# A hybrid decoder trunk on one Trainium2 core: V's first half in a transpose bank, a reordered first unit, and ScalarE's attention program without a loop

## What is computed

```python
q = (xn @ w_q).reshape(B, S, N_HEADS, HEAD_DIM).transpose(0, 2, 1, 3)
...
s = jnp.einsum('bhqd,bhkd->bhqk', q[:, :, q0:q1], k[:, :, :q1]) * scale
s = s + c[:, :, q0:q1, None] - c[:, :, None, :q1]
s = jnp.where(mask, s, -jnp.inf)
p = jax.nn.softmax(s, axis=-1)
outs.append(jnp.einsum('bhqk,bhkd->bhqd', p.astype(v.dtype), v[:, :, :q1]))
```

## Time and profile before

| | |
|---|---|
| median of 3 runs | 2560.55 us (2559.9 to 2560.63) |
| the profiled execution's own time | 2558.25 us |
| its span, first to last instruction | 2556.4 us |
| PE busy (matmuls) | 2446.8 us, 96% |
| DVE, ACT, POOL busy | 1271.8, 786.1, 124.8 us |
| granted TensorE clock, mean | 0.980 of full speed |
| attention, first score to last product | about 1166 to 1702 us |

### The profile page before, as it was taken

How to read it: one execution, slowest core, us unless ns; L and a number is a source line. 1 busy time by engine, 2 the same in 40 slices (tenths; PEclk the granted TensorE clock), 3 DMA queues, 4 the chain that set the end, 5 groups by cost and what they waited for, 6 DMA issues and landing times.

```text
span 2556.4 us, 28698 instructions
## 1 busy us (share of the span) xinstructions
PE 2446.8 (96%) x11353; PEld 2009.7 (79%) x11353; DVE 1271.8 (50%) x1257; ACT 786.1 (31%) x1045; POOL 124.8 (5%) x80
## 2 busy tenths in 40 slices
PE   7999889999999999998999999979999999999998
PEld 5788768888888888867777777767788888888887
DVE  5767674434333434466665656553434444444344
ACT  4543542111111111145555555542211111111112
POOL 1000010000000000011110111001000000000001
PEclk9999999999999999999999999979999999999999
DMA  3111011111111111120111101021211111111111
GB/s 116 58 58 49 25 33 50 49 49 46 44 49 49 49 49 49 34 83 25 34 34 34 33 26 32 25 85 55 58 50 49 49 43 47 49 49 49 49 33 66
DMA packets 167166, 122.63 MB, mean 48 GB/s; under 512 B 5072, under 2 KB 148672, under 8 KB 167104
## 3 DMA queue, kind: packets, MB, share of 16 engines
q1 hardware_dynamic: 165360, 117.52, 15.1%
q10 hardware_dynamic: 1744, 4.32, 0.6%
HBM read 113.37 MB, written 8.45 MB: 48 GB/s over the span
## 4 chain that ended last, share of the span: by engine, by line
PE 88%; DVE 5%; ACT 3%; issue 3%; ACTq 1%; DMA 0%; POOL 0%; DVEq 0%
PE ps L619 66%; PE ps L804 8%; PE ps L915 3%; PE ps L851 3%; PE ps L838 2%; PE ps L819 1%; PE ps L667 1%; PE ps L816 1%; ACT kh L1190 1%; DVE rstd L1346 1%; DVE kv_tmp L1716 0%; PE ps L663 0%; DVE wl L1316 0%; DVE resid L1359 0%; ACT kh L1195 0%
## 5 line engine op out<-in xcount | busy, mean ns | idle before, releaser
L619 PE MATMUL ps<-xh,wh 128*128 128x512 f32 x1680 | 523.5, 393 | 10.6 <-DVE wl L1316 10.1
L619 PE MATMUL ps<-xl,wh 128*128 128x512 f32 x1680 | 518.2, 390 | 0.0
L619 PE MATMUL ps<-xh,wl 128*128 128x512 f32 x1680 | 518.0, 389 | 0.0
L619 PEld LDWEIGHTS ps<-xh,wh 128*128 128x128 f32 x1680 | 315.1, 188 | 81.4 <-issue 16.4
L1353 DVE TENSOR_TENSOR tmp<-ps,rstd 128x1024 f32<-128x1024 f32 x96 | 117.3, 1224 | 506.0 <-PE ps L619 506.0
L619 PEld LDWEIGHTS ps<-xh,wl 128*128 128x128 f32 x1680 | 315.7, 188 | 65.9
L619 PEld LDWEIGHTS ps<-xl,wh 128*128 128x128 f32 x1680 | 315.7, 188 | 65.7
L1359 DVE TENSOR_TENSOR resid<-ps,resid 128x1024 f32<-128x1024 f32 x216 | 261.6, 1222 | 187.9 <-PE ps L619 187.5
L974 ACT ACTIVATE wh<-raw 128x1024 fp32r<-128x1024 f32 x193 | 201.6, 1049 | 402.2 <-PE ps L619 349.7
L1316 DVE TENSOR_TENSOR wl<-raw,wh 128x1024 fp32r<-128x1024 f32 x193 | 238.8, 1241 | 169.6 <-ACT wh L974 169.5
L619 PE MATMUL ps<-hh,wh 128*128 128x512 f32 x704 | 219.4, 393 | 1.7 <-DVE hl L1585 1.7
(11 more groups left out here) (186 smaller groups left out, 2792.2 us busy)
## 6 DMA issues: line engine op xcount, KB each, us to landing
raw<-in_w_ffn_in SPq DMA_DIRECT2D x88, 512.0 KB, 3.8
raw<-in_w_ffn_out SPq DMA_DIRECT2D x44, 512.0 KB, 3.3
raw<-in_w_rec_in SPq DMA_DIRECT2D x16, 512.0 KB, 4.0
raw<-in_w_kvf SPq DMA_DIRECT2D x16, 512.0 KB, 3.9
xin<-in_x SPq DMA_DIRECT2D x4, 1024.0 KB, 10.1
raw<-in_w_rec_out SPq DMA_DIRECT2D x8, 512.0 KB, 4.0
raw<-in_w_q SPq DMA_DIRECT2D x8, 512.0 KB, 3.7
spill<-resid SPq DMA_DIRECT2D x8, 512.0 KB, 2.6
```

The source lines that it names most:

```text
L619: last = pe.matmul(acc[:, h], w, v[:, h], start=(first and p == 0), stop=(final and p == 2))
```

## The change

Three things change. First, step A projects into `t_ps[0]` in place of `f_alt`. PE's waits ahead of A and ahead of S1 go; instead PE waits for DVE's scaling of A ahead of T0 of the first unit, the next user of that bank. Second, the first unit's steps stand in another order: T1 comes ahead of X and Y, and S0 and S1 of the next unit's scores come ahead of V1 and T3. Third, ACT's loop over the six middle pairs becomes a Python loop, so that its instructions stand one after the other six times with constants in place of registers. The loops of PE, DVE, POOL and SP stay.

```diff
 UNIT_STEPS = [
-    "T0 X Y T1 p p p V0 T2 p V1 T3 S0 p V2 S1 V3",
+    "T0 T1 X Y p p p V0 T2 S0 p V1 S1 T3 p V2 V3",
...
-        f_alt = ps[0][:, BANK:2 * BANK]
...
         def f_bank(step):
-            return f_alt if step in "aA" else f_ps
+            return t_ps[0] if step == "A" else f_ps
...
             def pair(i, uses, with_p=True):
                 p = f = 0
-                read = {"a": f_before(i) - 1, "f": f_before(i)}
+                read = {"f": f_before(i)}
                 for u, step in pair_steps(with_p):
                     m = int(step[1]) if len(step) > 1 else 0
                     if step in "AB":
-                        half, bank = ("AB".index(step), "af"["AB".index(step)])
-                        pe.wait_ge(f_drained, read[bank])
+                        half = "AB".index(step)
+                        if step == "B":
+                            pe.wait_ge(f_drained, read["f"])
                         for k in range(KT):
                             projection_part(f_bank(step), uses["V"], half, k, v_filled)
                         f += 1
-                        read[bank] = f_before(i) + f
+                        read["f"] = f_before(i) + f
...
                     elif step[0] == "S":
-                        if m == 1 and u == -1:
-                            pe.wait_ge(f_drained, read["a"])
...
                     elif step[0] == "T":
+                        if (u, m) == (0, 0):
+                            pe.wait_ge(f_drained, f_before(i) + 1)
                         transposes(i, u, m)
...
             pair(0, att_uses(0))
-            with act.Fori(0, (PAIRS - 2) // 2) as it:
+            for it in range((PAIRS - 2) // 2):
                 for d in range(2):
-                    pair(it * 2 + (d + 1), att_uses(None, it, d))
+                    pair(it * 2 + d + 1, att_uses(None, it, d))
```

## The result

The changed kernel takes **2537.64 us** (median of four runs, 2534.71 to 2540.91), the kernel before 2560.59 us in the same comparison: a ratio of 0.9913 with a 95% interval of 0.9901 to 0.9924, or 23 us less. The forecast was 2539.3 us with a range of 2533.5 to 2547.0. The profiled execution took 2534.71 us, with a span of 2532.9 us.

The account below looks back on a forecast made before the run. PE, busy 96% of the span, was taken as the bound, so only its idle or slow-clock time counts: -10.9 (A's bank) - 10.9 (ACT's jumps) + 0.6 (pair 7) = -21.2 us, from 2560.55 to 2539.3 us; range 2533.5 to 2547.0.

Parts of the forecast that it names:

- first matmul of A, pair 0, to B of pair 1: Attention's start: pair 1's share, about 1.6 us, of the 10.9 us of PE waits ahead of S1 goes.
- B of pair 1 to B of pair 7: Pairs 1 to 6: 409.81 us become 389.6, 20.2 less, from S1's waits (9.3) and ACT's jumps (10.9).
- B of pair 7 to the end: Last pair: the reordered first unit, without p steps as cover, costs 0.6 us more.
- A's bank: A in the transpose bank: seven PE waits ahead of S1 for DVE's scaling of A go, -10.9 us.
- the sentence on the new wait: T0 of the first unit: its new wait for A's scaling is met some 5 us before T0 is due.
- A pair's length: Pairs 1 to 6: without S1's wait and the jump each takes 66.75 - 1.82 = 64.93 us.
- ACT's jumps: ACT's loop written out: two jumps back, each costing 5.5 us in idle PE and slow matmuls, go, -10.9 us.
- The rival by which the 3.7 us are the broadcast's: ACT at pair boundaries: stall comes from rinv's broadcast, not the jump, and stays; 2550.2 us; chance 0.09, in part or whole.
- The slower rival: Written-out ACT: fetches meet the broadcast at n boundaries, 5.5 us each; 2577.7 us with all seven; chance 0.03.
- The first unit: Reordered steps in seven pairs: stall moves from next T0 to V3, idle time to ahead of V0; gain 0.
- Pair 7: First unit without p: V0 to next T0, 4.85 us before, gets 0.6 us longer.

Follow-up runs that it names:

- second profile of before: The kernel before, unchanged, profiled again: 2561.2 us, and 412.3 us from B of pair 1 to B of pair 7 (409.8 in its first profile).
- b_free: The changed kernel, with B waiting only for the previous projections' drains and not for A's scaling: 2534.4 us, ratio to before 0.9899.
- part two alone: The kernel before with only ACT's loop over the six middle pairs written out: 2547.2 us, ratio 0.9946.
- the fastest kernel: b_free with the first unit as T0 T1 X Y p p p p V0 T2 V1 T3 S0 S1 p V2 V3: 2522.5 us, ratio to before 0.9852.
- old_unit: The changed kernel with the first unit's steps in their old order: 2537.1 us, ratio to before 0.9910.
- part one alone: The kernel before with only A moved to the transpose bank and PE's waits as in the change: 2547.8 us, ratio 0.9951.
- Part three alone: The kernel before with only the new order of the first unit's steps: 2560.3 us, ratio 0.9999.

## Why the prediction was right, and where it wasn't

**The whole.** The forecast was 21.2 us less; the medians give 23.0. Between the two profiled executions it is 2558.25 - 2534.71 = 23.5 us, of which 1158.88 - 1156.74 = 2.1 us had passed before the changed part began. The 21.4 that remain fall like this:

| stretch | forecast | measured |
|---|---|---|
| first matmul of A, pair 0, to B of pair 1 | -1.6 | -1.7 |
| B of pair 1 to B of pair 7 | -20.2 | -18.9 |
| B of pair 7 to the end | +0.6 | -0.8 |

That the sum comes so near is in part luck: the six pairs gave 1.3 us less than forecast, and the end 1.4 us more. What lies between 21.4 and the 23.0 of the medians isn't explained. Both profiled executions are faster than their medians, by 2.3 and 2.9 us, and the four runs of the changed kernel spread over 6.2 us. The second profile of before shows how such a spread comes about: it holds slow matmuls in pairs 1 and 2 that the first lacked, behind waits that the change removes.

**A's bank.** The waits ahead of S1 went, and T0 and the exponential were covered by B as worked out. What failed is the sentence on the new wait: I named T0's and held that it was met before it was reached, and overlooked that `read["f"]` counts A's drain for B too. B waits in seven pairs; b_free shows that this costs 0.64 us a pair, 3.9 us in the six. It is in the diff, not in the profile of before, and reading the count that each wait asks for would have shown it.

**A pair's length.** I took 64.93 us, as 66.75 less the 1.82 in the bracket. Without any wait at the start it is 387.09 / 6 = 64.51 us, so the wait of 1.82 us cost 2.24, as far as pairs of two kernels can be set against each other. That error and B's wait went opposite ways, and 65.16 us came out: the sum was closer than its terms.

**ACT's jumps.** The mechanism holds, and the size within what two profiles of the same kernel differ by: 10.9 us in the six pairs with part two alone (13.5 against the second profile of before), one stall for each jump, 9.6 us (11.8 by the medians) when the loop is put back into the fastest kernel. What was too neat is the division: alone, the two parts gave 9.3 and 10.9 us of the six pairs, together (old_unit) 18.6, and by the medians 13.5 and 14.0 against 22.9. The likely reason is that they share slow matmuls behind gaps that each of them shortens; B of pair 5, 7.33 us before and 5.72 with part one alone, is such a case. The rival by which the 3.7 us are the broadcast's is wrong as to the cause and right as to some 1.1 us of the length. The slower rival, stalls all along a written-out program, didn't appear: ACT waits unnamed ahead of L1207 once, for 1.0 us. From 1000 to 1720 us the instruction queue q14 brought 14 packets, 21 before. The Trainium skill's account in "Runtime: NRT & Kernel Launch" (section "Instruction fetch mechanics"), a taken branch to code outside the fetched window that waits for a fetch, agrees with ACT, whose stalls of 3.4 to 4.2 us go with the jump and have an instruction packet in them where I looked; that DVE with a body of the same two pairs is through its jump in 0.3 us is not explained by any run here and stays open.

**The first unit.** Counted from V0 I had put the maximum at 3.04, the exponential at 3.50, `ptl`'s end at 5.2, V3 at 5.2 and the next T0 at 5.7 us. The rows of the changed kernel give 3.05, 3.51, 5.04, 5.10 and 5.61. The 0.6 us of idle time ahead of V0 is 0.59 to 0.63 in pairs 1 to 6. Part three alone and its removal both show no difference.

**Pair 7.** From V0 to the next T0 it takes 1637.41 - 1632.18 = 5.23 us, 4.85 before: +0.4 where I said +0.6. Yet the pair as a whole got 0.9 us shorter (62.96 against 63.88 us from B to the first matmul of L915), with less PE work at the lower clock: the mean granted clock of that stretch is 0.90, and 0.81 before. I had priced the pair's waits and not its clock. Over all profiles of this study the stretch takes 62.7 to 65.4 us at clocks of 0.80 to 0.90: 62.8 us (0.87) with part three alone, 62.7 (0.87) with parts one and two, 64.1 (0.82) and 63.9 (0.81) with part one and part two by themselves. No one part goes with it, and the cause stays open.

## What to carry to other kernels

When one stall ends in another engine's program order, follow the moved step through every engine that walks the same list: here a max and an exponential moved forward by 1.5 us made two copies wait behind them, and the gain came with an order that put the copies ahead of both and gave the idle time ahead of V0 other work. After merging two counters or banks, write down for each wait which event its count asks for. A loop's jump back can hold up an engine for longer than its other waits in that stretch while the profile names no releaser for it; put one turn outside the loop to see whether the stall goes with it.

## What the runs showed of the hardware

A jump back of ScalarE's loop over two pairs stalled it for 3.4 to 4.2 us, of which about 2.6 us remain when the 0.5 MB of transfers started just ahead of it are cut to an eighth; VectorE's took 0.3 us at the same place. By the lengths of the pairs with and without it, a wait of 1.82 us ahead of a matmul cost 2.24 us, and one shown as 0.35 to 0.45 cost 0.64. In pair 2 of the kernel before, TensorE idles for 1.82 us ahead of S1 in both profiles, after matmuls at the full clock. In the first the clock stays at 1.00 and B takes 5.50 us; in the second the mean granted clock from S1 to the end of B is 0.80 and B takes 6.08 us. So the clock behind a gap of that size wasn't the same in each execution, and a price read from one profile of this kernel carries some 2.5 us of that in the six pairs.
